# Six more 128-column quadrants turned by transposing DMAs instead of TensorE, in a float32 convolution-and-MLP layer

## What is computed

```python
h = rmsnorm(x, mix_norm)
b_gate, c_gate, v = split(h @ w_in, 3)           # w_in: 2048 x 6144
u = c_gate * v
y = depthwise causal convolution of u, 3 taps
x = x + (b_gate * y) @ w_out                     # 2048 x 2048
a = relu(rmsnorm(x, mlp_norm) @ w1)              # 2048 x 8192
x = x + (a * a) @ w2                             # 8192 x 2048
```

## Time and profile before

| | us |
|---|---|
| median of 3 runs | 1896.21 (1895.91 to 1896.45) |
| profiled execution | 1895.67 |
| its span, first to last instruction | 1893.9 |
| granted TensorE clock, mean | 1.000 |

### The profile page before, as it was taken

One profiled execution on the slowest core, in us unless ns is written; L12 is line 12 of the kernel. 1 busy time (PEld: TensorE's weight loads), 2 busy tenths in 40 slices (PEclk: granted clock), 3 DMA queues, 4 the chain that ended last, 5 costly groups with the idle time before them and its releaser, 6 DMA issues.

```text
span 1893.9 us, 22247 instructions
## 1 busy us (share of the span) xinstructions
PE 1885.1 (100%) x8476; PEld 1561.7 (82%) x8476; DVE 1677.6 (89%) x1500; ACT 1060.2 (56%) x1134; POOL 150.9 (8%) x242
## 2 busy tenths in 40 slices
PE   9999999999999999999999999999999999999999
PEld 8888888888888888888888888888888888888887
DVE  6688999899999898989989899898998889788878
ACT  6474664755548577586675866755444333433332
POOL 0100011000011111120111201100000000000000
PEclk9999999999999999999999999999999999999999
DMA  9795768859677966887968879699988878877783
GB/s 370 262 289 146 268 215 317 258 142 357 198 204 287 351 239 209 321 295 238 362 221 316 294 239 363 223 398 401 359 342 342 337 289 315 353 308 283 293 327 119
DMA packets 153946, 542.05 MB, mean 286 GB/s; under 512 B 44528, under 2 KB 48624, under 8 KB 128880
## 3 DMA queue, kind: packets, MB, share of 16 engines
q1 hardware_dynamic: 119712, 416.85, 57.9%
q0 software_dynamic: 33984, 123.75, 21.4%
q10 hardware_dynamic: 144, 0.04, 0.0%
HBM read 438.35 MB, written 94.37 MB: 281 GB/s over the span
## 4 chain that ended last, share of the span: by engine, by line
PE 93%; DVE 4%; issue 1%; DMA 1%; ACT 0%; SPq 0%; DVEq 0%; ACTq 0%
PE pair L1324 87%; PE pair L1337 5%; PE pair L1355 2%; DVE ring L1022 1%; DMA raw<-in_turns 1%; DVE raw L1016 1%; DVE sum_l_mix L1053 0%; DVE sum L1053 0%; DVE sum L1051 0%; DVE sum_first_mix L1065 0%; DVE quads L920 0%; DVE stage L1003 0%; ACT ring L663 0%; DVE sum_l_mix L1065 0%; DVE sum_first_mix L1053 0%
## 5 line engine op out<-in xcount | busy, mean ns | idle before, releaser
L1324 PE MATMUL pair<-ring,act 128*128 128x512 f32 x7728 | 1765.4, 390 | 2.5 <-DVE ring L1022 1.4
L1324 PEld LDWEIGHTS pair<-ring,act 128*128 128x128 f32 x7728 | 1447.0, 188 | 304.3 <-issue 5.3
L663 ACT ACTIVATE ring<-raw 128x1024 fp32r<-128x1024 f32 x659 | 695.5, 1058 | 758.6 <-PE pair L1324 480.1
L1022 DVE TENSOR_TENSOR ring<-raw,ring 128x1024 fp32r<-128x1024 f32 x659 | 791.4, 1221 | 153.5 <-ACT ring L663 151.7
L1016 DVE TENSOR_TENSOR raw<-raw 128x1024 f32<-128x1024 f32 x312 | 367.8, 1220 | 9.4 <-DMA raw<-in_turns 1.2
L530 POOL DMA_DIRECT2D spill<-stage x136 | 78.6, 617 | 486.4 <-ACT stage L802 370.9
L543 POOL DMA_DIRECT2D raw<-in_turns x56 | 50.4, 1053 | 696.2 <-DVE raw L1016 696.2
L1003 DVE TENSOR_TENSOR stage<-quads,stage 128x1024 fp32r<-128x1024 f32 x68 | 83.1, 1222 | 24.7 <-ACT stage L802 23.1
L1337 PE MATMUL pair<-ring,act 128*128 128x512 f32 x384 | 87.6, 390 | 1.2 <-DVE ring L933 1.2
L1337 PEld LDWEIGHTS pair<-ring,act 128*128 128x128 f32 x384 | 71.9, 188 | 16.5 <-issue 1.6
L802 ACT ACTIVATE stage<-quads 128x1024 fp32r<-128x1024 f32 x68 | 71.5, 1051 | 15.9 <-DVE quads L920 6.9
(11 more groups left out here) (109 smaller groups left out, 539.9 us busy)
## 6 DMA issues: line engine op xcount, KB each, us to landing
raw<-in_turns SPq DMA_DIRECT2D x191, 1024.0 KB, 7.4
act<-spill SPq DMA_DIRECT2D x290, 512.0 KB, 6.8
spill<-stage POOLq DMA_DIRECT2D x136, 512.0 KB, 9.3
act<-act_kept SPq DMA_DIRECT2D x74, 512.0 KB, 8.6
raw<-in_turns POOLq DMA_DIRECT2D x56, 512.0 KB, 8.6
act_kept<-act POOLq DMA_DIRECT2D x28, 512.0 KB, 9.8
x_tok<-in_x SPq DMA_DIRECT2D x4, 1024.0 KB, 14.1
x<-mixed SPq DMA_DIRECT2D x8, 512.0 KB, 15.5
```

Source lines behind the costliest of these rows:

```text
L663: nc.scalar.activation(ring[g % RING][:, 0], raw[:, raw_of(v, s), 2 * (s % 2):2 * (s % 2) + 2, :], ACT.Copy).then_inc(hi_ready, 1)
L1022: nc.vector.tensor_tensor(ring[g % RING][:, 1], raw[:, raw_of(v, s), 2 * (s % 2):2 * (s % 2) + 2, :], ring[g % RING][:, 0].bitcast(F32), A ...
L1324: mm = nc.tensor.matmul(bank, stationary, moving, start=(opens and k == 0 and n == 0), stop=(closes and k == NT - 1 and n == 2))
```

## The change

The fourth quadrant (m = 3) of the GATE pairs 2 and 5 and of the MIXED pairs 6 and 7 is turned by a transposing DMA, and so are m = 2 and m = 3 of the last UP pair 15, which before had all four on PE. In the last pair both transfers use one room at `ACTS2` (where `x11` comes later): the second waits on SP until the first has been joined. The load of `x11` waits on SP for the last quadrant. The direct splits and forms of stages 12 and 16 move by about one slot, and S3's split to slot 0 of the next stage. In GATE pairs DVE multiplies the joined quadrant at slot 9 instead of slot 7. Core of the diff:

```diff
 def by_transfer(q):
-    return 2 if KINDS[q] == GATED else int(KINDS[q] == UP and q < NQP - 1)
+    return 2 if KINDS[q] == GATED else 1 + int(q == NQP - 1)
...
-    DIRECT_SPLIT.update({(_v, 8): (_d, L11), (_v, 9): (_d, S1), (_v, 11): (_d, S2), (_v, 12): (_d, L12),
-                         (_v, 13): (_d, S3), (_v + 1, 1): (_d, S4), (_v + 1, 3): (_d, L22)})
-    DIRECT_FORM.update({(_v, 8): (_d, (0,)), (_v, 10): (_d, (1,)), (_v, 11): (_d, (2,)), (_v, 12): (_d, (3,))})
+    DIRECT_SPLIT.update({(_v, 7): (_d, L11), (_v, 10): (_d, S1), (_v, 12): (_d, S2), (_v, 13): (_d, L12),
+                         (_v + 1, 0): (_d, S3), (_v + 1, 1): (_d, S4), (_v + 1, 3): (_d, L22)})
+    DIRECT_FORM.update({(_v, 9): (_d, (0,)), (_v, 11): (_d, (1,)), (_v, 12): (_d, (2,)), (_v, 13): (_d, (3,))})
...
+                        if q == NQP - 1 and n > TRANSFERS[q]:
+                            sp.wait_ge(merged, 2 * (JOINED[q] + 1))
                         sp.dma_start_transpose(...)
...
+            def take_mixed_planes(q):
+                join_planes(q, quad["L21"])
+                act.wait_ge(merged, 2 * (JOINED[q] + 1))
+                for i in range(NT):
+                    tile = MLP + NT * (q - MIX0) + i
+                    o = quad["L21"][:, i, :]
+                    ins = nc.scalar.activation(o, o, ACT.Copy, scale=cols[:, tile:tile + 1])
+                ins.then_inc(quad_ready, 1)
...
-                        if kind == UP and s in (3, 5, 6):
+                        if kind == UP and s in (3, 5, 6) and not (v == V_DOWN and s == 6):
                             square_quad(q - 1, {3: 0, 5: 1, 6: 2}[s])
-                        if kind == UP and by_transfer(q - 1) and s == 5:
+                        if kind != GATED and by_transfer(q - 1) == 1 and s == 5:
                             put_planes(q - 1, 3)
-                        if kind == UP and s == 7 and not by_transfer(q - 1):
-                            square_quad(q - 1, 3)
...
+                        if v == V_DOWN and s in (4, 7):
+                            put_planes(q - 1, {4: 2, 7: 3}[s])
+                        if v == V_DOWN and s in (8, 11):
+                            square_planes(q - 1, {8: 2, 11: 3}[s])
+                        if kind == GATE and s == 8:
+                            join_planes(q - 1, joined[:])
+                        if kind == MIXED and s == 8:
+                            take_mixed_planes(q - 1)
...
-                        if kind == MIXED and s in (3, 5, 6, 7):
-                            take_mixed(q - 1, {3: 0, 5: 1, 6: 2, 7: 3}[s])
-                        if kind == MIXED and s in (4, 8, 10, 11):
-                            square_mixed(q - 1, *{4: (1, 0), 8: (2, 1), 10: (0, 2), 11: (3, 3)}[s])
+                        if kind == MIXED and s in (3, 5, 6):
+                            take_mixed(q - 1, {3: 0, 5: 1, 6: 2}[s])
+                        if kind == MIXED and s in (4, 9, 10, 11):
+                            square_mixed(q - 1, *{4: (1, 0), 9: (2, 1), 10: (0, 2), 11: (3, 3)}[s])
...
+            def gate_joined(q):
+                dve.wait_ge(merged, 2 * (JOINED[q] + 1))
+                dve.wait_ge(y_step, 2 * FORMED_U[q])
+                o = quad["L21"]
+                nc.vector.tensor_tensor(o, joined[:], o, ALU.mult).then_inc(quad_ready, 1)
```

More of the change, by code:

```diff
@@ L87 @@
     TRANSFERS.append(TRANSFERS[-1] + by_transfer(_q))
+JOINED = [sum(KINDS[p] != GATED for p in range(q)) for q in range(NQP + 1)]
 RECTIFIED = [8 * sum(k in (GATE, UP) for k in KINDS[:q]) for q in range(NQP + 1)]
@@ L283, in conv_mlp_layer @@
         planes_out = sem("planes_out")
-        planes_in = [sem(f"planes_in{i}") for i in range(3)]
+        planes_in = [sem(f"planes_in{i}") for i in range(4)]
         merged = sem("merged")
@@ L669, in place_read @@
                     act.wait_ge(u_formed, FORMED_U[q] + (2, 4, 2, 4)[m])
+                elif m < 4 - by_transfer(q):
+                    act.wait_ge(quad_turned, TURNED[q] + m + 1)
                 else:
-                    act.wait_ge(quad_turned, TURNED[q] + m + 1)
+                    act.wait_ge(planes_out, 2 * TRANSFERS[q + 1])
                 if KINDS[q] == MIXED:
@@ L724, in put_planes @@
                             act.wait_ge(spilled[i], 16 * stage_uses(1, i))
+                elif KINDS[q] == MIXED:
+                    act.wait_ge(added, pair_added(q) + FINISHED[m])
                 else:
                     act.wait_ge(rectified, RECTIFIED[q] + 2 * m + 2)
-                first, _, _, _, _, l22 = sums_of(q)
-                held = first if KINDS[q] == GATED and m == 0 else l22
+                    act.wait_ge(y_step, 2 * FORMED_U[q])
+                    if q == NQP - 1:
+                        product_done(act, V_DOWN - 1, L11)
+                        if m == 3:
+                            act.wait_ge(planes_in[3], 16)
+                first, _, _, _, s4, l22 = sums_of(q)
+                held = first if KINDS[q] == GATED and m == 0 else s4 if m == 2 else l22
                 words = held[:].bitcast(U16).rearrange("p t (b c z) -> p z b t c", c=P, z=2)
@@ L735, in turned_words, with join_planes, square_planes @@
                 return planes_t[plane_set(q, m)][:, 2 * NT * z:2 * NT * (z + 1)]
-            def square_planes(q):
-                act.wait_ge(planes_in[2], 16 * (q - UP0 + 1))
+            def join_planes(q, o, m=3):
+                if q == NQP - 1:
+                    act.wait_ge(planes_in[3], 16 * (m - 1))
+                else:
+                    act.wait_ge(planes_in[2], 16 * (JOINED[q] + 1))
                 quads_free(act, q)
-                o = quad["L21"]
                 words = o.bitcast(U16).rearrange("p a (t z) -> p z (a t)", z=2)
                 for z in range(2):
-                    nc.scalar.activation(words[:, z], turned_words(q, 3, z).rearrange("p a t -> p (a t)"),
+                    nc.scalar.activation(words[:, z], turned_words(q, m, z).rearrange("p a t -> p (a t)"),
                                          ACT.Copy).then_inc(merged, 1)
-                act.wait_ge(merged, 2 * (q - UP0 + 1))
+            def square_planes(q, m):
+                o = quad[{2: "L12", 3: "L21"}[m]]
+                join_planes(q, o, m)
+                act.wait_ge(merged, 2 * (JOINED[q] + (m - 1 if q == NQP - 1 else 1)))
                 o = o.rearrange("p a t -> p (a t)")
                 nc.scalar.activation(o, o, ACT.Square).then_inc(quad_ready, 1)
+            def take_mixed_planes(q):
[6 more added lines that the diff above has]
+                ins.then_inc(quad_ready, 1)
             def by_channels():
@@ L1212, in _ @@
                 for s in range(SLOTS):
-                    gated_late = v < V_DOWN and v % 2 == 0 and KINDS[q - 1] == GATE and s in (5, 6, 7)
-                    if gated_late:
-                        gate(q - 1, {5: 1, 6: 2, 7: 3}[s])
+                    gated_late = v < V_DOWN and v % 2 == 0 and KINDS[q - 1] == GATE and s in (5, 6, 9)
+                    if gated_late and s == 9:
+                        gate_joined(q - 1)
+                    elif gated_late:
+                        gate(q - 1, {5: 1, 6: 2}[s])
                     split_turn_lo(v, s)
```

17 lines of the change are left out of this document (11 added, 6 removed).

## The result

The changed kernel takes **1912.76 us** (median of 5 runs, 1912.0 to 1913.97) against 1896.21 (1895.57 to 1896.45); the ratio is 1.009, 95% interval 1.0077 to 1.0104. It is slower by 16.5 us; 1902.0 was forecast. Its profiled execution has a span of 1912.2 us at a granted clock of 1.000, so the clock is no part of it.

The account below looks back on a forecast made before the run. PE was taken to bound the kernel, with ACT and DVE becoming the bound in stages 14 to 17. Terms -0.25 - 2.2 + 4.5 + 4.5 - 0.45 = +6.1 us gave 1902.3, put at 1902.0, range 1899 to 1905.5.

Parts of the forecast that it names:

- What bounds the kernel: Whole span: PE is busy for all but 9 us, so anything that makes PE wait adds in full.
- Stage 12: Pair 5: a gain of 2.2 us; a turn and a 0.48 us stall go, DVE and ACT enter stage 14 earlier.
- Stages 14 and 15, 16 and 17: MIXED pairs 6 and 7: losses of 4.5 us each, as ACT's put and join make ACT and DVE late.
- DVE cannot catch up: Stages 14 and 15: DVE has nothing but work up to 640.03, so its lateness stays, +4.5 us.
- the wait for landing: Costs nothing in stages 14 and 16, put and join nearly 8 us apart; up to 1.4 us in 6 and 12.
- the order of put and take: Slot 5 of stages 14 and 16: planes put ahead of taking m = 1 make PE wait about 1.2 and 1.75 us.
- Stages 6 to 8: Pair 2: nearly nothing, -0.25 us, bounds -1.7 and +0.9; the chain leaves PE over a 16.44 us weight load.
- Stage 32: Pair 15: two turns save 1.75 us, waits at slots 6 and 8 leave -0.45; SP's blocked loads make it.
- The Trainium skill's page: Prefers TensorE for 128x128 transposes; about 1.3 us per DMA block, 21 us per transfer; forecast trusted the trace's 4.3 median.
- A: All of the added work is hidden: six turns and two waits go, -5.8 us, 1890.4; chance 0.08.
- B: Stages 14 to 17: the ring absorbs the lateness, only the wait for the take remains, -2.8 us, 1893.4; chance 0.20.
- C: Stages 6 and 33: transfers or SP's blocked loads also land late, +0.9 and +1.7 us, 1905; chance 0.12.

Follow-up runs that it names:

- gate5: Kernel before with only m = 3 of pair 5 by DMA, stage 12's direct splits about a slot later: 1893.83 us.
- table12: Kernel before with only the moved direct splits and forms of stage 12, all quadrants turned as before: 1894.92 us.
- mixed_pairs: The change limited to m = 3 of MIXED pairs 6 and 7 by DMA, the other pairs as in the kernel before: 1906.02 us.
- table16: Kernel before with only the later order of direct splits and forms in stage 16: 1897.23 us.
- take_first: Whole changed kernel, but ACT takes m = 1 before putting the planes of m = 3 in slot 5 of stages 14 and 16: 1912.65 us.
- gate_pairs: The change limited to m = 3 of GATE pairs 2 and 5 by DMA, the other pairs as in the kernel before: 1895.64 us.
- last_pair: The change limited to last pair 15, m = 2 and m = 3 by DMA through one room, otherwise the kernel before: 1902.01 us.
- mixed_small_squares: mixed_pairs with m = 1 taken before the put, and squares of m = 0, 2 and 3 reading 32 of 512 columns: 1904.18 us.
- mixed_old_table: mixed_pairs with the direct splits and forms of stage 16 in the order of the kernel before: 1906.59 us.
- mixed_dve_relief: mixed_pairs with less DVE work, nine additions in stages 13, 15 and 17 cut to 64 of 512 columns: 1902.82 us.
- last_on_act: last_pair with both transposing DMAs issued by ACT in its own queue instead of by SP: 1906.31 us.

## Why the prediction was right or wrong

**What bounds the kernel**: right. PE's waits rose by 17.5 us, from some 5 to 22. The six turns gave back 4.9 (0.80 each, the last 0.91, where the forecast took 0.87), and the waits cost some 4 more than their idle time (last section), in all +16.6.

**Stage 12**: right, -2.1 in the change, and gate5 has -2.3 us by itself. The forecast gave all of it to the transfer and the waits it removes; by table12 0.8 to 1.1 us of it belong to the moved direct splits. But it is PE that gained the 2.1. The forecast had PE gain 1.35 and DVE and ACT 0.8 more, a lead that would shorten the third turn's wait in stage 14 to 1.2 us. That wait was 1.93, and 2.02 in mixed_pairs, which has no gain in stage 12: the lead was not there.

**Stages 14 and 15, 16 and 17**: right in direction, place and engine. Forecast +9.0, measured +10.0 alone and +10.5 inside the change. The step behind it, that DVE cannot catch up, is the one that six kernels bear out. Too small was stage 16: the wait at slot 12 was put at 1.6 and measured 2.1, that at slot 12 of stage 17 grew by 1.4; table16 puts about 1 us on the moved splits, which the forecast had counted only as a relief for the copy of S3. One step failed here too: the wait for landing was to cost "nothing in stages 14 and 16". In stage 14 it cost nothing; in stage 16, where the DMA engines were full, the landing took 9.2 us and ACT waited 1.28. The emphasis on the order of put and take was wrong: take_first changed it and won nothing.

**Stages 6 to 8**: -0.25 was forecast, and gate_pairs less gate5 is +1.8 us, twice the upper bound, though the intervals of the two overlap. The failed step was to look for a late landing of the transfer only. It landed in time; late was the weight load behind it, for whose 16.44 us the forecast had a lower value in mind but no higher one. In gate_pairs it was issued at 284.23 and used at 303.59, 19.4 us.

**Stage 32**: the step that failed most. -0.45 (bounds -1.75 and +0.5) against +6.0 in last_pair. Two terms: the landing was taken from the other transfers, 3.7 to 6.2 us, though none of those was issued behind so many bytes (from 1277 to 1290 before, the DMA share was 1.02 at 420 GB/s, a row that was at hand). It was 9.8 us, and 9.5 in last_pair, and ACT's wait for the shared room was not in the sum at all; and SP's blocked loads "make it" with 7 to 10 us of landing. R11 was issued at 1319.17 instead of about 1301, took 12.5 us, and ACT waited 5.98 us for it.

**The sum**: the GATE pairs 2.1, the MIXED pairs 1.0 and the last pair 6.4 us above the forecast, 9.5 of the 10.5 us by which the whole missed. The other 1.0 is within the intervals of the medians.

**The range.** It was said to come from the bounds of the terms, 1899 to 1905.5. Those bounds add up to 1896.6 and 1906.7, so the stated range was narrower than its own working, and both lie under the 1912.8 measured.

**The Trainium skill's page** that the prediction weighed ("VectorE: DVE Perf Modes") came out right in its advice and not by its price: here the loss is ACT's copies and the held queues, and a whole transfer still lands in 4.3 us in the median. The price of one block stands in that page's section "The three transpose paths".

**The rivals.** A is out: none of the MIXED or last pair's cost was hidden. B is out: by the table, what DVE waited more came out in the time, and the ring's four slots absorbed none of it. C named the right place and had the wrong price, 1905, since it took the landing as 6.2 and the load as 16.4 us and had nothing for ACT's wait for the room.

**The best version** is gate5, 1893.83 us, 0.12% under the kernel before, with an interval that ends just under 1. By the 0.2% that the forecast called measurable it is no change. Each of the other groups of transfers costs more than its turns save: pair 2 by 1.8 us, the MIXED pairs by 10.0, the last pair by 6.0.

## What to carry to other kernels

A turn on the busiest engine costs 0.8 to 0.9 us here; handed to a chain ACT, DMA, ACT it costs 4.5 us of ACT, and what matters is not ACT's 56% but whether it and the engine between it and TensorE (here DVE) have spare time in that stage. Before adding a transposing DMA, read the DMA share and the GB/s of the stretch in which it is issued. At a share of 1.0 here the issue held its engine for 3.3 to 5.2 us where the engines moved under 200 GB/s and for 7.4 to 12.7 us where they moved some 400, and everything behind it in its queue was late. And price an order of instructions and a transfer each by itself: a third to a half of the gain in stage 12 needed no transfer.

## What the hardware showed

- The issue of one 512 KB transposing DMA (one quadrant) held its engine 1.6 us at least and 2.0 to 2.5 in the median of a kernel. Where the DMA engines were full it held 3.3 to 5.2 us in stages 4, 8 and 10, 5.3 to 7.4 in stage 16, and in stage 32 7.4 to 12.7 on SP and 10.3 on ACT. The share alone does not tell these apart: in the kernel before, 178 to 181.4 reads 1.13 at 174 GB/s, and 1277 to 1290 reads 1.02 at 420; one plain load took 0.3 to 3.3 there.
- A wait costs about 0.27 us more than its idle time. Of the three rows below, the first is from before and the others from the changed kernel:

```profile
249.44 5.70 PE L1324 MATMUL pair<-ring,act 128*128 128x512 f32 x24
306.14 5.72 PE L1370 MATMUL pair<-ring,act 128*128 128x512 f32 x24 [0.82 <-DVE ring L1057]
312.95 11.16 PE L1370 MATMUL pair<-ring,act 128*128 128x512 f32 x48 [1.08 <-DVE ring L1057]
```

  The 24 matmuls behind a wait take no longer than the 24 without one: a row runs to the end of its last matmul, and in unbroken work the next one has started before that. So two slots advance PE by 5.46 us, but where a wait follows they take 5.72 and then the idle time: 6.81 from 306.14 to 312.95, with 1.08 idle. With some 15 new waits that is 4 us of the 16.5, a term that the forecast had not.
- TensorE's granted clock fell behind some waits, and the length of the wait alone does not tell which. The changed kernel, with waits up to 2.11 us, keeps 1.00 (2.4 GHz). Behind 1.83 us in mixed_small_squares 725 to 730 reads 0.74, behind 2.61 in mixed_old_table 690 to 695 reads 0.66, and behind 2.76 in mixed_dve_relief 660 to 665 reads 0.66, part of each at 2.4 and part at 1.2 GHz. Each cost 1.4 to 1.6 us (a slot of 2.84 us behind a wait took 4.26, the turn 1.67 in place of 1.06). In last_on_act PE stood 8.5 us, and the two stretches above read 0.89 and 0.76.
